# The first addition of a chunk's down products, moved between the two taps of a gate row on VectorE

## The chip, the cores and the metric

The kernel runs on one core of a Trainium2 chip. The metric is the device time of one execution in microseconds (us); the median of repeated executions counts, and lower is better.

## What is computed

One layer of a streaming encoder: an input projection, three token mixers (windowed pooling, a chunked state-space scan, stick-breaking attention), an output projection and layer norm, then a gated channel mixer beside a gated per-layer embedding, and a last layer norm. The change lies in the channel mixer:

```python
def conv_glu_ffn(x, w_up, conv_w, conv_b, w_down):
    up = causal_depthwise_conv(x @ w_up, conv_w, conv_b)     # width 3 along the 1024 tokens
    gate, val = up[..., :D_FF], up[..., D_FF:]               # D_FF = 2816
    return (jax.nn.silu(gate) * val) @ w_down
```

with x of 1024 tokens by 1024 features, all float32.

## The kernel before

The channel mixer's 2816 hidden features are 22 row tiles of 128, taken in 11 chunks (c = 0 to 10) of two tiles, called pp = 0 and 1. A tile needs a gate row (r = 0) and a value row (r = 1), each 128 features by 1024 tokens. The four 512-wide quarters of this up projection come out of seven products (A11, S1, S2, S3, A12, S4, A22: a Strassen scheme), so VectorE has to combine them in PSUM: five `combine` steps per tile. Every product and every down product is a float32 product made of three passes: each operand is held as a rounded part (`hi`) and a rest (`lo`). ScalarE writes the `hi` part of each weight operand (`op_hi`), VectorE the `lo` part (`op_lo`), GpSimd the sums of weight tiles (`weight_sums`).

The program is written by hand, engine by engine, as straight-line queues tied by semaphores. Each engine runs its own queue in order. Chunks 2 to 8 run in a hardware loop (`Fori`), in which the wait values and the columns of the tap weights come from registers; chunks 0, 1, 9 and 10 are written out.

**TensorE** in chunk c (`chunk`, from line 1189): six products of tile 0 (`even`), then the 16 down products of chunk c-1 (`down(c, k)`, k = 0 to 15), then A22 of tile 0, then seven products of tile 1 (`odd`). A down product is two hidden tiles times three passes, six matmuls of 512 columns (L735 to L737 in the profile); a product of `even` or `odd` is twelve (L1094 to L1096). The down products go to four PSUM banks in turn. Down product k, from k = 4 on, therefore waits until addition k-4 has emptied its bank:

```python
if k >= 4:
    eng.wait_ge(dn_added, 16 * (c - 1) + k - 3 + 16 * it)
```

**VectorE** in chunk c runs `chunk` (line 2045 on). `add_down(c, ks, it)` (L1989) adds the down products ks from PSUM to the accumulator `acc` in SBUF; each addition waits for its down product (`dn_full`) and counts up `dn_added`. `taps(c, pp, r, it, parts)` makes the last two taps of the width-3 convolution of one row: part 1 (L1937) waits for ScalarE's first tap (`row_tap`, L1519) and counts up `row_mid`, part 2 (L1941) waits for `row_mid` and counts up `row_done`. Both read PSUM and `conv_ff` (the SBUF buffer `cf`) and write `conv_ff`. `combine` steps 1 to 5 are L1965, L1968, L1971, L1973, L1975; `op_lo` is L603; `glu` L1948; `h_low` L1954.

Who waits for the gate row's `row_done` (`taps(c, 0, 0)`): ScalarE's `silu(c, 0)` (L1525), which stands in ScalarE's queue behind `op_hi` of A11, S1 and S2 of tile 1; and TensorE's first product of chunk c+1.

Of the kernel before, what the change touches and what calls it, by code (L numbers as in the profile page):

```python
# [293 lines left out]
def build(nc, ctx, a, out):  # L294
# [305 lines left out]
    def op_lo(c, o, pp, it=0):  # L600

        nc.vector.wait_ge(op_hi_done, lo_count(c, o, pp) + 18 * it)
        nc.vector.tensor_tensor(op_place(c, o, pp, True), op_raw(c, o, pp), op_place(c, o, pp, False).bitcast(F32),  # L603
                                ALU.subtract).then_inc(op_lo_done, 1)

    def up_row(pp, r):

        b = (Y_BANK if r else X_BANK)[pp]
        return ps[:, b:b + 2, :].rearrange("p b n -> p (b n)")
# [1030 lines left out]
    def _(eng):  # L1640
# [286 lines left out]
        def column(c, step, it):  # L1927
            return par[:, c:c + 1] if isinstance(it, int) else par[:, bass.ds(c + step * it, 1)]

        def taps(c, pp, r, it=0, parts=(1, 2)):  # L1930

            t = 2 * pp + r
            src = up_row(pp, r)
            w = PARAMS["ff_w"] + 3 * (4 * c + t)
            if 1 in parts:
                eng.wait_ge(row_tap, 4 * c + t + 1 + 4 * it)
                v.scalar_tensor_tensor(out=cf[:, r, 1:], in0=src[:, :S - 1], scalar=column(w + 1, 12, it),  # L1937
                                       in1=cf[:, r, 1:], op0=ALU.mult, op1=ALU.add).then_inc(row_mid, 1)
            if 2 in parts:
                eng.wait_ge(row_mid, 4 * c + t + 1 + 4 * it)  # L1940
                v.scalar_tensor_tensor(out=cf[:, r, 2:], in0=src[:, :S - 2], scalar=column(w, 12, it),  # L1941
                                       in1=cf[:, r, 2:], op0=ALU.mult, op1=ALU.add).then_inc(row_done, 1)

        def glu(c, pp, it=0):

            eng.wait_ge(silu_ff, 2 * c + pp + 1 + 2 * it)
            eng.wait_ge(row_done, 4 * c + 2 * pp + 2 + 4 * it)
            v.tensor_tensor(cf[:, 0, :], cf[:, 0, :], cf[:, 1, :], ALU.mult).then_inc(glu_done, 1)  # L1948

        def h_low(c, pp, it=0):  # L1950

            eng.wait_ge(hh_done, 2 * c + pp + 1 + 2 * it)
            h_h, h_l = (h2h, h2l) if c == LASTC else (hh, hl)
            v.tensor_tensor(h_l[pp][:, :], cf[:, 0, :], h_h[pp][:, :].bitcast(F32), ALU.subtract).then_inc(h_done, 1)  # L1954

        def combine(c, pp, step, it=0):

            n = 10 * c + 5 * pp
            x, y = X_BANK[pp], Y_BANK[pp]
            p1, u2 = pu[:, 0, :], pu[:, 1, :]  # L1960
            product = {1: S2, 2: S1, 3: S3, 4: S4, 5: A22}[step]
            eng.wait_ge(prod_full, product_count(c, product, pp) + 14 * it)
            if step == 1:
                eng.wait_ge(p1_done, 2 * c + pp + 1 + 2 * it)
                ins = v.tensor_tensor(u2, p1, ps[:, y + 1, :], ALU.add)  # L1965
            elif step == 2:
                eng.wait_ge(combined, n + 1 + 10 * it)
                ins = v.tensor_tensor(p1, u2, ps[:, x + 1, :], ALU.add)  # L1968
            elif step == 3:
                eng.wait_ge(combined, n + 2 + 10 * it)  # L1970
                ins = v.tensor_tensor(ps[:, y + 1, :], p1, ps[:, y, :], ALU.add)  # L1971
            elif step == 4:
                ins = v.tensor_tensor(ps[:, x + 1, :], u2, ps[:, x + 1, :], ALU.add)  # L1973
            else:
                ins = v.tensor_tensor(ps[:, y, :], u2, ps[:, y, :], ALU.add)  # L1975
            ins.then_inc(combined, 1)

        def add_down(c, ks, it=0):

            first = 16 * (c - 1)  # L1980
            for k in ks:
                j, h = k // 2, k % 2
                eng.wait_ge(dn_full, first + k + 1 + 16 * it)
                dst = acc[:, j, h * HALF:(h + 1) * HALF]
                if k == 0:
                    eng.wait_ge(u_free, 2 * KT)
                    if first:
                        eng.wait_ge(dn_added, first + 16 * it)
                v.tensor_tensor(dst, dst, ps[:, DOWN_BANKS[k % 4], :], ALU.add).then_inc(dn_added, 1)  # L1989
# [38 lines left out]
        def second_half(c, it=0):  # L2028

            op_lo(c + 1, S2, 0, it)  # L2030
            op_lo(c + 1, S3, 0, it)
            combine(c, 1, 4, it)
            op_lo(c + 1, A12, 0, it)
            taps(c, 1, 0, it)
            combine(c, 1, 5, it)
            op_lo(c + 1, S4, 0, it)
            taps(c, 1, 1, it)
            if c + 1 < LASTC:
                op_lo(c + 1, D0A, 0, it)
            glu(c, 1, it)  # L2040
            if c + 1 < LASTC:
                op_lo(c + 1, D1A, 0, it)
            h_low(c, 1, it)

        def chunk(c, it=0):

            combine(c, 0, 1, it)
            combine(c, 0, 2, it)
            op_lo(c, D0B, 0, it)
            combine(c, 0, 3, it)  # L2050
            op_lo(c, D1B, 0, it)
            op_lo(c, A22, 0, it)
            combine(c, 0, 4, it)
            taps(c, 0, 0, it)
            add_down(c, range(5), it)
            op_lo(c, A11, 1, it)
            add_down(c, range(5, 8), it)
            op_lo(c, S1, 1, it)
            op_lo(c, S2, 1, it)
            add_down(c, range(8, 16), it)  # L2060
            op_lo(c, S3, 1, it)
            op_lo(c, A12, 1, it)
            combine(c, 0, 5, it)
            op_lo(c, S4, 1, it)
            taps(c, 0, 1, it)
            op_lo(c, A22, 1, it)
            glu(c, 0, it)
            h_low(c, 0, it)
            op_lo(c + 1, A11, 0, it)
            combine(c, 1, 1, it)  # L2070
            combine(c, 1, 2, it)
            op_lo(c + 1, S1, 0, it)
            combine(c, 1, 3, it)
            second_half(c, it)

        first_chunk()
        second_half(0)
        chunk(1)
        with eng.Fori(0, CHUNKS - 4) as it:
            chunk(2, it)  # L2080
        chunk(LASTC - 1)
        c = LASTC
        combine(c, 0, 1)
# [275 lines left out]
```

## Time and profile before

| | us |
|---|---|
| median of 3 runs | 1300.06 (1298.59 to 1300.7) |
| the profiled execution | 1299.85 |
| its span in the trace | 1298.1 |
| TensorE matmul busy | 1260.1 (97%) |
| VectorE busy | 839.7 (65%) |
| ScalarE busy | 512.9 (40%) |
| GpSimd busy | 232.7 (18%) |
| the 144 additions L1989 on VectorE | 96.1 busy, 685 ns each |
| the 44 taps of part 1 and the 44 of part 2 | 56.4 busy each, 1281 and 1282 ns each |

The span is what the profiler sees of one execution; 1.75 us lie around it. In the trace PE is a matmul, PEld a weight load, DVE VectorE, ACT ScalarE, POOL GpSimd. A time in brackets behind a row is how long the engine was idle before it, and the arrow says what ended that. The end of a matmul is modelled: in a dense stream a matmul of 512 columns is shown with 0.39 us, while the next one starts 0.227 us after it. In the same way the next VectorE instruction starts slightly before the shown end of the one before it.

### The profile page before, as it was taken

The page shows a single profiled execution, that of the slowest core. Times are in us where ns is not written, and L with a number is a line of the kernel's source. Part 1 is how long each engine was busy: PE and PEld are TensorE (multiplying, and loading weights), DVE is VectorE, ACT ScalarE, POOL GpSimd, SP SyncE. Part 2 cuts the span into 40 slices and gives each one's busy share as a digit, 9 for nine tenths or more (in the row PEclk, how much of TensorE's full clock was granted, in tenths as well). Part 3 has the DMA queues.
Part 4 walks back from the last instruction along what each step waited for, and adds up shares of the span by engine and source line. Part 5 has one row for each costly group of instructions (what it writes and reads, how often), then busy time and mean ns, then how long its engine had stood idle before and what let it go on. Part 6 is the DMA issues. An engine that isn't in the chain of part 4 may idle for free.

```text
span 1298.1 us, 16439 instructions
## 1 busy us (share of the span) xinstructions
PE 1260.1 (97%) x6120; PEld 1013.9 (78%) x6120; DVE 839.7 (65%) x1004; ACT 512.9 (40%) x794; POOL 232.7 (18%) x157
## 2 busy tenths in 40 slices
PE   7999999999998999999989999999999999999997
PEld 6777777777876888888868887878788877878886
DVE  5546646646495546625677777767686777687774
ACT  5435545457764225213433342424232423233441
POOL 0000000062300002610311111111111121212127
PEclk9999999999999999999989999999999999999999
DMA  6101101100004122110120211111111212010112
GB/s 240 49 33 37 36 26 46 36 34 17 1 18 136 58 78 84 50 34 17 65 65 33 65 49 48 48 48 65 34 64 51 75 35 65 32 65 33 65 62 117
DMA packets 22804, 71.94 MB, mean 55 GB/s; under 512 B 2528, under 2 KB 2784, under 8 KB 22752
## 3 DMA queue, kind: packets, MB, share of 16 engines
q1 hardware_dynamic: 22752, 71.22, 16.1%
q8 instruction: 36, 0.59, 0.2%
q14 instruction: 16, 0.13, 0.0%
HBM read 67.02 MB, written 4.19 MB: 55 GB/s over the span
## 4 chain that ended last, share of the span: by engine, by line
PE 54%; DVE 16%; issue 7%; ACT 5%; DMA 4%; POOL 2%; DVEq 1%; ACTq 0%; SPq 0%; POOLq 0%
PE ps L735 12%; PE ps L737 12%; PE ps L736 12%; DVE conv_ff L1937 4%; DVE w_lo L603 3%; DMA raw<-u_up 3%; ACT conv_ff L1519 2%; PE ps L1094 2%; PE ps L1096 2%; PE ps L1095 2%; ACT w_hi L598 2%; PE ps L813 1%; PE ps L830 1%; DMA down_raw<-u_down 1%; POOL weight_sums L2251 1%
## 5 line engine op out<-in xcount | busy, mean ns | idle before, releaser
L735 PE MATMUL ps<-x_hi,w_hi 128*128 128x512 f32 x336 | 139.1, 414 | 8.3 <-DVE x_lo L1691 7.3
L1094 PE MATMUL ps<-mix_hi,w_hi 128*128 128x512 f32 x352 | 139.0, 395 | 7.5 <-DVE partial L1968 6.3
L1096 PE MATMUL ps<-mix_hi,w_lo 128*128 128x512 f32 x352 | 138.0, 392 | 0.0
L1095 PE MATMUL ps<-mix_lo,w_hi 128*128 128x512 f32 x352 | 138.0, 392 | 0.0
L737 PE MATMUL ps<-x_hi,w_lo 128*128 128x512 f32 x336 | 132.4, 394 | 0.0
L736 PE MATMUL ps<-x_lo,w_hi 128*128 128x512 f32 x336 | 131.8, 392 | 0.0
L1989 DVE TENSOR_TENSOR acc<-acc,ps 128x512 f32<-128x512 f32 x144 | 96.1, 685 | 49.7 <-PE ps L737 49.0
L2251 POOL TENSOR_TENSOR weight_sums<-raw 128x512 f32<-128x512 f32 x22 | 32.4, 1475 | 480.4 <-DMA raw<-u_up 480.4
L735 PE MATMUL ps<-h_hi,w_hi 128*128 128x512 f32 x288 | 113.2, 393 | 5.2 <-DVE acc L1989 5.1
L736 PE MATMUL ps<-h_lo,w_hi 128*128 128x512 f32 x288 | 112.2, 390 | 0.0
L737 PE MATMUL ps<-h_hi,w_lo 128*128 128x512 f32 x288 | 112.1, 389 | 0.0
L598 ACT ACTIVATE w_hi<-weight_sums 128x512 fp32r<-128x512 f32 x44 | 27.8, 631 | 206.4 <-PE ps L737 157.9
L1094 PE MATMUL ps<-t_hi,w_hi 128*128 128x512 f32 x264 | 102.8, 389 | 0.3 <-DVE ps L1971 0.3
L1096 PE MATMUL ps<-t_hi,w_lo 128*128 128x512 f32 x264 | 102.7, 389 | 0.0
L1095 PE MATMUL ps<-t_lo,w_hi 128*128 128x512 f32 x264 | 102.7, 389 | 0.0
L1519 ACT ACTIVATE conv_ff<-ps,params 128x1024 f32<-128x1024 f32 x44 | 53.1, 1206 | 97.5 <-DVE ps L1975 54.8
L1715 DVE TENSOR_TENSOR_SCAN ps<-ps,zero 128x1024 f32<-128x1024 f32 (+7 forms) x48 | 65.3, 1361 | 33.3 <-ACT ps L1298 33.2
L1094 PEld LDWEIGHTS ps<-mix_hi,w_hi 128*128 128x128 f32 x352 | 66.6, 189 | 24.8 <-DVE partial L1968 5.7
L735 PEld LDWEIGHTS ps<-x_hi,w_hi 128*128 128x128 f32 x336 | 63.7, 189 | 23.9 <-DVE x_lo L1691 7.3
L1096 PEld LDWEIGHTS ps<-mix_hi,w_lo 128*128 128x128 f32 x352 | 66.6, 189 | 14.2
L1937 DVE SCALAR_TENSOR_TENSOR conv_ff<-ps,params,conv_ff 128x1023 f32<-128x1023 f32 x44 | 56.4, 1281 | 33.0 <-ACT conv_ff L1519 32.9
L1095 PEld LDWEIGHTS ps<-mix_lo,w_hi 128*128 128x128 f32 x352 | 66.6, 189 | 13.7
(268 smaller groups left out, 2727.7 us busy)
## 6 DMA issues: line engine op xcount, KB each, us to landing
raw<-u_up SPq DMA_DIRECT2D x44, 512.0 KB, 3.3
raw<-u_in SPq DMA_DIRECT2D x22, 512.0 KB, 3.3
down_raw<-u_down SPq DMA_DIRECT2D x38, 256.0 KB, 2.7
x_stage<-u_x SPq DMA_DIRECT2D x8, 512.0 KB, 8.4
raw<-u_out SPq DMA_DIRECT2D x8, 512.0 KB, 3.2
x_nat<-x_nat SPq DMA_DIRECT2D x8, 512.0 KB, 3.2
raw<-u_gate SPq DMA_DIRECT2D x8, 512.0 KB, 3.3
out<-o_norm SPq DMA_DIRECT2D x7, 512.0 KB, 2.6
```

The costliest lines, as they stand in the source:

```text
L598: nc.scalar.activation(op_place(c, o, pp, False), op_raw(c, o, pp), ACT.Copy).then_inc(op_hi_done, 1)
L735: mm(dst, w_hi, x_hi, start=first, stop=False)
L736: mm(dst, w_hi, x_lo, start=False, stop=False)
L737: return mm(dst, w_lo, x_hi, start=False, stop=last)
L1094: mm(dst, w_h[:, k], t_h[:, kt, :], start=fresh and kt == 0, stop=False, skip_group_check=True)
L1095: mm(dst, w_h[:, k], t_l[:, kt, :], start=False, stop=False, skip_group_check=True)
L1096: last = mm(dst, w_l[:, k], t_h[:, kt, :], start=False, stop=kt == 3, skip_group_check=True)
L1519: act(cf[:, r, :], up_row(pp, r), ACT.Identity, scale=column(w, 12, it), bias=column(b, 4, it)).then_inc(row_tap, 1)
L1715: link(v.tensor_tensor_scan(z[:, ::-1], z[:, ::-1], zero[:, 0:1].broadcast_to([P, keys]), 1.0, ALU.mult, ALU.add))
L1937: v.scalar_tensor_tensor(out=cf[:, r, 1:], in0=src[:, :S - 1], scalar=column(w + 1, 12, it), in1=cf[:, r, 1:], op0=ALU.mult, op1=ALU.add). ...
L1989: v.tensor_tensor(dst, dst, ps[:, DOWN_BANKS[k % 4], :], ALU.add).then_inc(dn_added, 1)
L2251: g.tensor_tensor(t0[:, :], wb[:, 0:HALF], wb[:, HALF:D], ALU.add).then_inc(sum_done, 1)
```

## The change

Within `chunk` on VectorE (chunks 1 to 9), `taps(c, 0, 0)` is split into its two parts, and addition 0 goes between them; additions 1 to 4 follow part 2. No instruction, wait or count is added or removed, and no other queue is touched.

```diff
             op_lo(c, A22, 0, it)
             combine(c, 0, 4, it)
-            taps(c, 0, 0, it)
-            add_down(c, range(5), it)
+            taps(c, 0, 0, it, (1,))
+            add_down(c, range(1), it)
+            taps(c, 0, 0, it, (2,))
+            add_down(c, range(1, 5), it)
             op_lo(c, A11, 1, it)
             add_down(c, range(5, 8), it)
```

## Rows read from the trace of the kernel before

**Rows 1.** The page: TensorE's busy share, granted clock in 40 slices.
```profile
PE 1260.1 (97%) x6120; PEld 1013.9 (78%) x6120; DVE 839.7 (65%) x1004; ACT 512.9 (40%) x794; POOL 232.7 (18%) x157
...
PEclk9999999999999999999989999999999999999999
```

**Rows 2.** Waits of PE: who for whom, us in total, times, longest.
```profile
PE ps L1094 <- DVE partial L1968: 6.3, 8, 4.6
PE ps L735 <- DVE acc L1989: 5.1, 7, 0.9
```

**Rows 3.** Timeline of chunk 3: start us, us, engine, line, operation.
```profile
790.80 1.28 DVE L1937 SCALAR_TENSOR_TENSOR conv_ff<-ps,params,conv_ff 128x1023 f32<-128x1023 f32 x1 [1.69 <-ACT conv_ff L1519]
792.24 1.28 DVE L1941 SCALAR_TENSOR_TENSOR conv_ff<-ps,params,conv_ff 128x1022 f32<-128x1022 f32 x1 [0.15 <-DVE conv_ff L1937]
792.29 0.19 PEld L735 LDWEIGHTS ps<-h_hi,w_hi 128*128 128x128 f32 x1
792.51 0.39 PE L735 MATMUL ps<-h_hi,w_hi 128*128 128x512 f32 x1
792.96 0.39 PE L737 MATMUL ps<-h_hi,w_lo 128*128 128x512 f32 x1
793.44 3.11 DVE L1989 TENSOR_TENSOR acc<-acc,ps 128x512 f32<-128x512 f32 x5
793.89 1.28 POOL L2251 TENSOR_TENSOR weight_sums<-raw 128x512 f32<-128x512 f32 x1 [24.78 <-DMA raw<-u_up]
794.17 0.50 PE L735 MATMUL ps<-h_hi,w_hi 128*128 128x512 f32 x1 [0.82 <-DVE acc L1989]
794.51 0.39 PE L736 MATMUL ps<-h_lo,w_hi 128*128 128x512 f32 x1
795.26 1.30 POOL L2255 TENSOR_TENSOR tables<-weight_sums,raw 128x512 f32<-128x512 f32 x1
796.47 0.69 DVE L603 TENSOR_TENSOR w_lo<-raw,w_hi 128x512 fp32r<-128x512 f32 x1
```

**Rows 4.** Timeline: down product 4 in chunks 2, 7 and 9.
```profile
732.67 0.50 PE L735 MATMUL ps<-h_hi,w_hi 128*128 128x512 f32 x1 [0.47 <-DVE acc L1989]
...
1039.97 0.50 PE L735 MATMUL ps<-h_hi,w_hi 128*128 128x512 f32 x1 [0.88 <-DVE acc L1989]
...
1161.77 0.39 PE L737 MATMUL ps<-h_hi,w_lo 128*128 128x512 f32 x1
1162.25 0.50 PE L735 MATMUL ps<-h_hi,w_hi 128*128 128x512 f32 x1
```

**Rows 5.** The chain of waits, from chunk 3 into chunk 4: start us, us, what.
```profile
813.28 0.24 PE ps L1096
813.54 0.71 DVE ps L1975
...
845.58 0.70 DVE partial L1968
```

**Rows 6.** Timeline of PE where S4 of tile 0 begins, chunk 4.
```profile
845.76 0.39 PE L1096 MATMUL ps<-mix_hi,w_lo 128*128 128x512 f32 x1
846.39 0.49 PE L1094 MATMUL ps<-mix_hi,w_hi 128*128 128x512 f32 x1 [0.25 <-DVE partial L1968]
```

**Rows 7.** Timeline of chunk 1, written out: taps and first additions.
```profile
668.67 1.28 DVE L1937 SCALAR_TENSOR_TENSOR conv_ff<-ps,params,conv_ff 128x1023 f32<-128x1023 f32 x1 [1.28 <-ACT conv_ff L1519]
669.99 1.28 DVE L1941 SCALAR_TENSOR_TENSOR conv_ff<-ps,params,conv_ff 128x1022 f32<-128x1022 f32 x1
```

**Rows 8.** Timeline of ScalarE, chunk 3, behind the gate row's taps.
```profile
799.94 0.63 ACT L598 ACTIVATE w_hi<-weight_sums 128x512 fp32r<-128x512 f32 x1 [8.78 <-PE ps L737]
...
801.00 1.05 ACT L1525 ACTIVATE conv_ff<-conv_ff 128x1024 f32<-128x1024 f32 x1
```

**Rows 9.** Timeline of chunk 2: a lo step beside GpSimd.
```profile
734.02 1.29 POOL L2255 TENSOR_TENSOR tables<-weight_sums,raw 128x512 f32<-128x512 f32 x1
734.97 0.89 DVE L603 TENSOR_TENSOR w_lo<-raw,w_hi 128x512 fp32r<-128x512 f32 x1
```

## The prediction

> **What bounds the kernel now.** I read the page first. TensorE is busy for 97% of the span at a granted clock of nearly full speed throughout (the 2.4 GHz level) [rows 1]. So there is little idle time to win, and the question is which of TensorE's few pauses this edit touches. The view of waits, for TensorE, answers it: in the channel mixer two waits return in nearly every chunk. The down products wait for an addition L1989, seven times, 5.1 us in all, and S4 of tile 0 waits for `combine` step 2 (L1968), eight times, of which one is 4.6 us (in chunk 1) and the other seven (6.3 - 4.6) / 7 = 0.24 us in the mean [rows 2].
>
> Which addition the down products wait for is seen in the timeline of chunk 3 [rows 3]. Four down products run without a break; the last matmul of number 3 starts at 792.96. The first matmul of number 4 would follow 0.227 us later, at 793.19, the spacing of the dense stream (792.51 to 792.96 is two such steps). It starts at 794.17. VectorE began the five additions 0 to 4 at 793.44; five in 3.11 us, with the last shown at its full 0.69 us, means one every 0.605 us. Addition 0 ends at 793.44 + 0.69 = 794.13, and TensorE starts 0.04 us later. So it is addition 0 that TensorE waits for, and addition 0 itself waits for nothing but its place in VectorE's queue: down product 3's last matmul starts at 792.96, so down product 0's last one, three times six matmuls before, started at 788.9. In front of it stand the two taps of the gate row, at 790.80 and 792.24.
>
> **The loss at this place.** In chunk 3 down product 4 starts 794.17 - 793.19 = 0.98 us late. The restart also costs something: the first matmul behind the pause is shown with 0.50 instead of 0.39 us, and the second one comes 0.34 instead of 0.227 us after it [rows 3], 0.11 us more. Together 1.09 us. The view's idle time (0.82) counts from the modelled end of the last matmul, so the loss is that number plus 0.39 - 0.227 = 0.16, plus 0.11: idle plus 0.27. The seven waits are chunks 2 to 8, from 0.47 (chunk 2) to 0.88 us (chunk 7) [rows 4]. Their sum is 5.1 + 7 x 0.27 = 7.0 us, a mean of 1.0 and a largest of 1.15. In chunk 9 the same gap is too short to show as idle: 1161.77 to 1162.25 is 0.48 instead of 0.227, so 0.25 + 0.11 = 0.36 us [rows 4]. In chunk 1 there is no such gap, since TensorE was held up 4.6 us shortly before [rows 2]. Total to be won here: 7.4 us, if nothing new takes the place.
>
> **The change, part by part.** It moves one addition over one tap; counts and durations stay. I write t for the start of part 1 of the taps (790.80 in chunk 3).
>
> Addition 0, moved forward. Back to back, the instruction behind a tap starts 793.44 - 792.24 = 1.20 us after it [rows 3]. So addition 0 starts at t + 1.20 and is done at t + 1.20 + 0.69 + 0.04 = t + 1.93 as TensorE sees it. Before it was t + 3.37. It is 1.44 us earlier: 792.73 in chunk 3, where TensorE's down product 4 is due at 793.19. Its weight load goes 0.22 us ahead of the matmul (792.29 before 792.51), so the wait should be met by 792.97, and is. In chunk 7, with the largest loss, the due time against the taps is 0.06 us sooner: still covered. The pause at down product 4 goes in all eight chunks.
>
> Part 2 of the taps, moved back by 0.605 us less what its own wait cost. In the loop it stands 1.44 us behind part 1 with 0.15 us idle for `row_mid` [rows 3]; in the written-out chunk 1 it is 1.32 us and nothing is shown as idle [rows 7]. With an addition between them the wait is met while VectorE works. So part 2 starts at t + 1.20 + 0.605 = t + 1.80 instead of t + 1.44, 0.36 us later. Who waits for `row_done`: silu (L1525), which runs 801.00, behind an `op_hi` that sat 8.78 us idle for a down product [rows 8]. The row would be done at 790.80 + 1.80 + 1.28 = 793.88, seven us ahead. TensorE's wait for it is in the next chunk. Price nothing; the cover is those seven us.
>
> Additions 1 to 4. Addition 1 starts at t + 1.80 + 1.20 = t + 3.00, done for TensorE at t + 3.73. Before, it was t + 2.64 + 0.605 = t + 3.25: it comes 0.25 us sooner too, by the vanished idle time at the tap. But down product 5 now falls due sooner as well: with loss L at number 4 gone, its first matmul is due at t + 3.37 + 0.11 + 1.36 - L = t + 4.84 - L (1.36 is six steps of 0.227). **Here lies the next wait.** With L = 1.09 it is due at t + 3.75, addition 1 is there at t + 3.73: met, but not the 0.22 us ahead that the weight load wants. I charge what the restart rows show, 0.11 us, so a loss of 3.73 + 0.11 - (4.84 - L) = L - 1.0 where that is positive: 0.15 in chunk 7, 0.09 in chunk 3, little or none elsewhere, 0.3 us in all. If the 0.15 us of idle at the tap remained after all, each of the seven chunks of the loop with a mean L of 1.0 would lose 0.15 more, 0.9 us in all, as the small loss of chunk 2 leaves it free. Down product 6 waits for addition 2, which comes 0.605 us after addition 1 and is due 1.36 us later: free, and so on.
>
> The lo step of A11 (L603, 796.47) stands behind addition 4, which can't start before down product 4 is done (793.19 + 1.36 + about 0.17, so 794.7) nor before t + 3.00 + 3 x 0.605 = 795.62. The lo step then starts at 796.22 instead of 796.47. It now meets GpSimd's L2255 (795.26 to 796.56) [rows 3]. What that does is seen in chunk 2: there the same step started beside L2255 (734.02 to 735.31) and took 0.89 instead of 0.69 us [rows 9]. The worst is that it waits for the whole rest of L2255 and ends at 796.56 + 0.69 = 797.25, 0.34 us late. Bounds 0 and 0.34 us on VectorE; addition 5 behind it then ends by about 798, and down product 9, the one that waits for it, is due at 794.55 + 4 x 1.36 = 800.0. Price on TensorE nothing, and the cover is 2 us.
>
> The Trainium skill (SBUF — State Buffer, section Who interferes with whom) says why: a VectorE instruction with two SBUF inputs contends with a GpSimd instruction that reads SBUF, and is blocked to its end, while one with at most one SBUF input is not. By that rule the lo step would wait until 796.56 and end at 797.25, the two taps and the additions (one tensor from PSUM each) would be untouched, and the sum would be the same. The five additions beside L2251 and L2255 at one per 0.605 us agree with it, and so does the 0.89 in chunk 2, roughly.
>
> **Does the gain last to the end?** What could eat it is a chain of fixed length that starts before the pause and ends behind it, past TensorE. The chain of waits shows what the next chunk hangs on: A22 of tile 0, TensorE's last matmul behind the down products (813.28), then `combine` step 5 (L1975), lo steps, a weight load, the sums, taps, down to step 2 (L1968) at 845.58 [rows 5], where S4 starts with 0.25 us shown as idle, a loss of 0.4 plus 0.11 us [rows 6]. Both this chain and TensorE's own stream start from the same matmul at 813.28, which comes after the down products. If the down products end 1 us sooner, both start 1 us sooner, and S4's pause stays as it is. The trace supports this: the pause at down product 4 varies from 0.47 to 0.88 us over the chunks [rows 4], while those at S4 are 0.24 in the mean, 0.25 in chunk 4 [rows 2, 6]; if it were the pause at S4 that gives way, the two would trade against each other. What is late next is then down product 5 with its few hundredths, and S4 as before. The other transfers and sums are released by counts of lo steps, which in this stretch are paced by TensorE (the 8.78 us of [rows 8]).
>
> The sum: 7.4 - 0.3 = 7.1 us off the profiled execution of 1299.85, hence 1292.8. The median of the runs is 0.2 us above that execution, so 1293.0. With the bound of 0.9 us it is 1293.9; with no new loss at all 1292.7. With the spread of the runs (1298.6 to 1300.7) this case's own range is 1291.5 to 1295.
>
> **The rivals.**
> The gain is won and half of it given back. A chain past TensorE that I took as moving along does not, for instance a weight transfer begun before the down products, and S4's pause grows from 0.5 to about 1 us in each loop chunk. Against it stands the constancy of the S4 pauses. Result 1293.0 + 8 x 0.45 = 1296.6.
>
> The change doesn't do what it says: TensorE's wait isn't ended by addition 0's place in the queue but by something that moves with it (down product 0's own count arriving late). Then addition 0 in its new place would wait as long as before and the time stays 1300. Against it: 0.04 us between the end of addition 0 and the matmul, and no idle time before it.
>
> Slower: contention on VectorE. Part 2 and addition 1 now run where GpSimd's L2251 starts (793.89). If GpSimd held them up as it holds up lo steps, until both its instructions end at 796.56, addition 1 would be ready at 796.56 + 0.69 + 0.04 = 797.29, and down product 5, which ran at 794.17 + 0.11 + 1.36 = 795.64 before, would be 1.65 + 0.11 us later than before: eight times that is +14 us, 1314. It decides against the change once addition 1 is ready later than t + 4.73, 1.0 us behind my estimate. Against it: the five additions ran undisturbed beside the same two instructions [rows 3].
>
> **How the numbers follow.** My case 0.84, half given back 0.07, no effect 0.05, slower 0.04. The likeliest gives 1293.0. The range takes the case with its bounds and reaches toward the half-absorbed one: 1291.3 to 1296.8. 0.2% of the time is 2.6 us, about what a measurement of this kernel can tell from no change. Faster by more (below 1297.5): my case and the half one, 0.90. Within: 0.06. Slower: 0.04.
>
> **What would show it.** In the trace after: in chunk 3 addition 0 starts 1.20 us behind part 1, part 2 0.6 us behind that with no idle shown; the waits of PE for L1989 fall from 5.1 us to under 0.5, and what is left sits at down product 5; a loop chunk lasts 60.4 us, measured between two lo steps of A11, instead of 796.47 - 734.97 = 61.5 [rows 3, 9]; the pauses at S4 stay near 0.24; the lo step of A11 takes up to 1.1 us with no TensorE pause behind it. I am wrong if the pauses at S4 grow by what the down products gained, if a pause of several tenths shows at down product 5, or if the chunk's length falls by less than 0.8 us.

## The result and the profile after

The changed kernel takes 1292.64 us in the median of six runs (1291.07 to 1295.67), against 1300.15 us before (1298.59 to 1300.7). The ratio is 0.9945, with a 95% interval of 0.9932 to 0.9958. A second set of five runs gives the same ratio. The forecast was 1293.0 us.

The page of the changed kernel, the line of the engines:

```profile
span 1290.5 us, 16439 instructions
PE 1257.5 (97%) x6120; PEld 1013.5 (79%) x6120; DVE 838.9 (65%) x1004; ACT 512.8 (40%) x794; POOL 232.4 (18%) x157
```

The same instructions run; the span is 7.6 us shorter. The view of waits, for PE and PEld, answers to [rows 2] (who for whom, us in total, times, longest):

```profile
PE ps L1094 <- DVE partial L1968: 6.3, 8, 4.6
...
PEld ps L735 <- DVE acc L1989: 1.8, 6, 0.5
```

The wait of matmuls for an addition (5.1 us before) has gone from the list; what is left of it is a wait of six weight loads, 1.8 us against 8.6 in eight before. The wait at S4 is unchanged to the tenth. The timeline of chunk 3 answers to [rows 3]:

```profile
788.80 1.28 DVE L1937 SCALAR_TENSOR_TENSOR conv_ff<-ps,params,conv_ff 128x1023 f32<-128x1023 f32 x1 [1.69 <-ACT conv_ff L1519]
790.00 0.68 DVE L1989 TENSOR_TENSOR acc<-acc,ps 128x512 f32<-128x512 f32 x1
790.59 1.28 DVE L1941 SCALAR_TENSOR_TENSOR conv_ff<-ps,params,conv_ff 128x1022 f32<-128x1022 f32 x1
791.20 0.39 PE L735 MATMUL ps<-h_hi,w_hi 128*128 128x512 f32 x1
791.78 2.47 DVE L1989 TENSOR_TENSOR acc<-acc,ps 128x512 f32<-128x512 f32 x4
792.33 0.39 PE L737 MATMUL ps<-h_hi,w_lo 128*128 128x512 f32 x1
792.52 0.19 PEld L735 LDWEIGHTS ps<-h_hi,w_hi 128*128 128x128 f32 x1 [0.22 <-DVE acc L1989]
792.56 0.46 PE L735 MATMUL ps<-h_hi,w_hi 128*128 128x512 f32 x1
793.21 1.29 POOL L2257 TENSOR_TENSOR tables<-weight_sums,raw 128x512 f32<-128x512 f32 x1
794.17 0.88 DVE L603 TENSOR_TENSOR w_lo<-raw,w_hi 128x512 fp32r<-128x512 f32 x1
```

Addition 0 starts 1.20 us behind part 1 of the taps, part 2 follows 0.59 us behind it without the 0.15 us of idle time. Down product 4 starts at 791.20 in a stream without a gap. The new place to look at is down product 5 at 792.56: its weight load waits for addition 1 (791.78 + 0.69 = 792.47). From tap to tap (chunk 3 to 4) a loop chunk now takes 849.41 - 788.80 = 60.61 us, against 61.42 before. Measured as the prediction asks, between the lo steps of A11 in chunks 2 and 3, it is 794.17 - 733.52 = 60.65 us: 0.85 less than before, where 1.1 were forecast for this chunk.

**Where the 7.6 us lie.** The stretch that the change can reach runs from chunk 1's down product 0 to TensorE's last matmul. These two rows of the timeline, for the changed kernel:

```profile
665.49 0.39 PE L735 MATMUL ps<-h_hi,w_hi 128*128 128x512 f32 x1
...
1282.17 0.39 PE L1134 MATMUL ps<-last_w_hi,last_h_lo 128*128 128x512 f32 x1
```

That is 616.68 us. Before, the same two stand at 666.46 and 1289.75, 623.29 us apart. So 6.6 us come from the stretch (0.3 of them because TensorE's first matmuls in it still ran at half the granted clock before, which the last section comes back to). Another 0.97 us were there before it began, in code that is the same, and the 8.3 us behind the last matmul are equal. From here on I compare this stretch first, and the medians beside it. What lies behind the last matmul is 8.3 us in the first three kernels of the table, 9.0 to 9.1 in the next four and 7.9 in the last two, so a median holds that difference too.

| kernel | stretch, us | lost at down products 4 and 5, chunks 2 to 9 | lost at S4, chunks 3 to 9 | median, us |
|---|---|---|---|---|
| before | 623.29 | 7.4 | 3.6 | 1300.15 |
| changed | 616.68 | 0.8 | 3.6 | 1292.64 |
| changed, once more | 616.07 | 0.3 | 3.6 | 1292.12 |
| `late` | 628.64 | 12.2 | 3.7 | 1305.56 |
| `two_between` | 615.80 | 0 | 3.6 | 1291.83 |
| `ahead` | 615.75 | 0 | 3.7 | 1291.65 |
| `tap_last` | 615.58 | 0 | 3.6 | 1292.57 |
| `s4_first` | 614.72 | 3.6 | 0 | 1287.62 |
| `s4_ahead` | 610.84 | 0 | 0 | 1283.51 |

A loss is what the distance between the starts of two matmuls has above 0.227 us, summed where it is over 0.03 us. The median of the kernel before was 1300.15 beside the first set of the changed kernel, 1300.27 beside the second set and the runs up to `ahead`, and 1299.73 beside the last three.

### The profile page after: what moved, and what is told of

Read it like the earlier page. It is cut to its first block, busy times and chain, and to the rows that moved or that the text cites. A ratio compares the mean times of both kernels' runs of the same rounds, so it can differ in the third digit from the quotient of the medians.

```text
span 1290.5 us, 16439 instructions
## 1 busy us (share of the span) xinstructions
PE 1257.5 (97%) x6120; PEld 1013.5 (79%) x6120; DVE 838.9 (65%) x1004; ACT 512.8 (40%) x794; POOL 232.4 (18%) x157
## 4 chain that ended last, share of the span: by engine, by line
PE 60%; DVE 13%; issue 6%; ACT 4%; DMA 2%; POOL 2%; DVEq 0%; ACTq 0%; POOLq 0%; SPq 0%
PE ps L735 13%; PE ps L737 13%; PE ps L736 13%; PE ps L1094 4%; PE ps L1095 3%; PE ps L1096 3%; DVE conv_ff L1937 3%; DMA raw<-u_up 2%; DVE w_lo L603 2%; ACT conv_ff L1519 2%; PE ps L813 1%; PE ps L830 1%; ACT w_hi L598 1%; PE ps L789 1%; POOL weight_sums L2253 1%
## 5 line engine op out<-in xcount | busy, mean ns | idle before, releaser
L736 PE MATMUL ps<-x_lo,w_hi 128*128 128x512 f32 x336 | 132.2, 393 | 0.0
```

What stands on the lines that cost most here:

```text
L736: mm(dst, w_hi, x_lo, start=False, stop=False)
```

## The experiments

**`after_again`: the changed kernel once more**, no edit.

> The changed kernel once more. The trace after shows 6.4 us gone from the tap of chunk 2 to the end, 0.15 in chunk 1, and another 1.0 us that was already there when chunk 1's tap began, in code that the change does not touch. Theory A: that 1.0 us is a variation between executions, the change is worth 6.6 us, so the ratio in time is near 0.9950, and this profile has its chunk 1 tap anywhere between 667 and 669 us. Rival B: the new order shifts something before chunk 1 too, the tap stands at 667.7 again and the ratio is 0.9942.

Median 1292.12 us (1290.55 to 1294.18), ratio 0.9945 (0.9931 to 0.9958). In its profile chunk 1's tap starts at 666.52, against 667.67 in the first profile of the same kernel and 668.67 before. The point moves by 1.1 us between two profiles of one kernel, and in the other kernels with nothing changed ahead of it, it stands between 666.5 and 668.0 (667.80 in `late`, whose edit leaves everything up to this point as before). So theory A holds in that the 1.0 us need no cause in the change. The ratio itself doesn't tell 0.9950 from 0.9942. The stretch was worth 7.2 us this time, mainly since down product 5 lost 0.3 instead of 0.8 us.

**`late`: addition 0 later still**, from the kernel before:

```diff
             taps(c, 0, 0, it)
-            add_down(c, range(5), it)
             op_lo(c, A11, 1, it)
+            add_down(c, range(5), it)
```

> The kernel before, with the lo step of A11 in front of addition 0 as well: addition 0 comes 0.6 us later behind both taps. Theory A (TensorE waits for addition 0's place in the queue, and every tenth lost there is lost to the end): the pause at down product 4 grows by 0.6 us in eight chunks, 4.9 us, so 1305.0 us. Rival B (the pause is ended by something else, or a later wait takes up the shift): no change, 1300.

Median 1305.56 us (1305.10 to 1306.13), ratio 1.0044 (1.0028 to 1.0059): 5.3 us slower, the stretch 5.35 us longer. The timeline of chunk 3:

```profile
792.44 1.28 DVE L1941 SCALAR_TENSOR_TENSOR conv_ff<-ps,params,conv_ff 128x1022 f32<-128x1022 f32 x1 [0.15 <-DVE conv_ff L1937]
793.63 0.68 DVE L603 TENSOR_TENSOR w_lo<-raw,w_hi 128x512 fp32r<-128x512 f32 x1
794.23 3.12 DVE L1989 TENSOR_TENSOR acc<-acc,ps 128x512 f32<-128x512 f32 x5
...
793.11 0.39 PE L737 MATMUL ps<-h_hi,w_lo 128*128 128x512 f32 x1
794.97 0.50 PE L735 MATMUL ps<-h_hi,w_hi 128*128 128x512 f32 x1 [1.47 <-DVE acc L1989]
```

One instruction of 0.60 us more in front of addition 0, and TensorE's idle time goes from 0.82 to 1.47 us [rows 3]. Theory A it is: TensorE waits for addition 0's place in VectorE's queue. The 0.4 us above the expected 4.9 are chunk 1, which I had left out: it had no pause before, and loses 0.64 us at down product 4 here. Every tenth lost at this place is lost to the end, in both directions.

**`two_between` and `ahead`: room for addition 1.** Two ways to have addition 1 ready sooner. `two_between`, from the changed kernel:

```diff
             taps(c, 0, 0, it, (1,))
-            add_down(c, range(1), it)
+            add_down(c, range(2), it)
             taps(c, 0, 0, it, (2,))
-            add_down(c, range(1, 5), it)
+            add_down(c, range(2, 5), it)
```

and, from the changed kernel as well,

```diff
-            taps(c, 0, 0, it, (1,))
             add_down(c, range(1), it)
-            taps(c, 0, 0, it, (2,))
+            taps(c, 0, 0, it)
             add_down(c, range(1, 5), it)
```

> The changed kernel, with addition 1 also between the two taps. The trace after shows a new loss at down product 5 of 0.05 to 0.31 us in six chunks, 0.76 us together, because addition 1 is ready just when its matmul is due. Theory A: addition 1 is now ready 1.2 us sooner, that loss goes, part 2 of the taps is 0.6 us later at no price: 0.7 us faster than the changed kernel. Rival B: part 2 of the taps has a price after all (silu, glu) and the time is the same or longer by up to 0.6 us in each of nine chunks.

> The changed kernel, with addition 0 in front of both taps, where VectorE sits idle 1.7 us for ScalarE's first tap. Theory A: addition 0 is done in that idle time, the pause at down product 4 goes as with the change, and addition 1 comes 2.6 instead of 3.0 us behind the first tap, so down product 5 is free as well: 0.7 us faster than the changed kernel, 1291.9. Rival B: addition 0's wait for down product 0 holds the taps up, in each chunk by up to 0.5 us, and some 4 us of the gain are lost: 1297.

Medians 1291.83 us (1291.62 to 1295.09; ratio 0.9942, 0.9928 to 0.9956) and 1291.65 us (1290.92 to 1292.43; ratio 0.9934, 0.9921 to 0.9948). The medians can't tell these from the changed kernel; the traces can. In both, no matmul of the down products starts late in any chunk, and the stretch is 0.9 us shorter than in the first profile of the changed kernel, 0.3 us shorter than in the second. The expected 0.7 lies between. In `ahead`, addition 0 used the idle time in front of the tap:

```profile
787.74 0.69 DVE L1989 TENSOR_TENSOR acc<-acc,ps 128x512 f32<-128x512 f32 x1 [0.36 <-PE ps L737]
789.08 1.28 DVE L1937 SCALAR_TENSOR_TENSOR conv_ff<-ps,params,conv_ff 128x1023 f32<-128x1023 f32 x1 [0.65 <-ACT conv_ff L1519]
```

It waited 0.36 us for down product 0 (the bracket), and 0.65 us were still idle before the tap. Rival B of `ahead` falls, and so does that of `two_between`, whose stretch is shorter and not longer.

**`tap_last`: the cover of part 2 tried out.**

```diff
             taps(c, 0, 0, it, (1,))
-            add_down(c, range(1), it)
+            add_down(c, range(5), it)
             taps(c, 0, 0, it, (2,))
-            add_down(c, range(1, 5), it)
```

> The changed kernel, with part 2 of the gate row's taps behind all of additions 0 to 4. Theory A (part 2 has some seven us of cover before silu): its row is done about 3 us later than with the change and nothing waits for it; additions 1 to 4 come 1.2 us sooner, so no loss at down product 5. From chunk 1's down product 0 to TensorE's last matmul: 615.8 us, as with addition 1 between the taps, 0.3 to 0.9 less than with the change. Rival B: the later row end is felt at silu, and what follows it, in every chunk: 617 or more.

Median 1292.57 us (1290.81 to 1293.26), ratio 0.9946 (0.9929 to 0.9962); stretch 615.58 us. Part 2 and who needs it, chunk 3:

```profile
792.27 1.28 DVE L1941 SCALAR_TENSOR_TENSOR conv_ff<-ps,params,conv_ff 128x1022 f32<-128x1022 f32 x1
...
795.74 0.64 ACT L598 ACTIVATE w_hi<-weight_sums 128x512 fp32r<-128x512 f32 x1 [7.81 <-PE ps L737]
796.28 0.62 ACT L598 ACTIVATE w_hi<-tables 128x512 fp32r<-128x512 f32 x1
796.80 1.05 ACT L1525 ACTIVATE conv_ff<-conv_ff 128x1024 f32<-128x1024 f32 x1
```

The row ends at 793.55, silu runs at 796.80, right behind two `op_hi`, of which the first waited for a down product. So part 2 has cover of 3.2 us even here. With the change it ends at 790.59 + 1.28 = 791.87 and silu runs at 798.03, so the cover is 6.2 us. Theory A holds.

**`s4_first`: the other pause taken away alone**, from the changed kernel:

```diff
# second_half(c), on VectorE; the same two are taken out where chunk c+1 began
+            combine(c + 1, 0, 1, it)
+            combine(c + 1, 0, 2, it)
             h_low(c, 1, it)
# chunk(c), and the written-out last chunk
-            combine(c, 0, 1, it)
-            combine(c, 0, 2, it)
```

> The changed kernel, with steps 1 and 2 of combine for chunk c+1 in front of h_low(c, 1) on VectorE, for the pause at S4 that the change left untouched (0.51 us in eight chunks). Theory A: step 2 comes 1.3 us sooner, the pause at S4 goes, but the taps stay where they are against the matmul A22 of tile 0, so TensorE reaches down products 4 and 5 0.5 us sooner than the additions allow: at least 0.4 of each 0.5 us is lost again there, and only chunk 1, with its long pause at S4, keeps about 1.2 us. 1291.0. Rival B: the pauses at S4 and at the down products are independent, all 4 us and the 1.2 of chunk 1 are kept: 1287.

Median 1287.62 us (1286.56 to 1288.83), ratio 0.9908 (0.9891 to 0.9924). In chunk 3:

```profile
787.92 0.50 PE L735 MATMUL ps<-h_hi,w_hi 128*128 128x512 f32 x1
788.26 0.40 PE L736 MATMUL ps<-h_lo,w_hi 128*128 128x512 f32 x1
...
789.19 0.39 PE L737 MATMUL ps<-h_hi,w_lo 128*128 128x512 f32 x1
789.71 0.50 PE L735 MATMUL ps<-h_hi,w_hi 128*128 128x512 f32 x1
```

Down product 5 starts 0.52 instead of 0.227 us behind the matmul before it, and the restart adds 0.11. In chunks 3 to 9 the 3.6 us lost at S4 are gone, and 3.6 us are lost at down products 4 and 5, where it was 0.3 to 0.8: over the loop theory A is what happened, the two pauses trade, and some 0.4 to 0.9 us are kept. As a time my 1291.0 was still a miss by 3.4 us, and 1287.62 is near the 1287 of rival B: the median alone would have spoken for the wrong theory. Chunk 1 and the last chunk made the difference: the long wait at S4 of chunk 1 falls from 4.6 to 2.9 us, and from chunk 9's down product 0 to the last matmul it takes 132.2 instead of 133.0 us. There it isn't S4 that gains, which in the last chunk has no pause in either kernel, but A22 of the second tile. In the changed kernel it waits for `combine` step 3 (L1971):

```profile
1228.79 0.50 PE L1094 MATMUL ps<-t_hi,w_hi 128*128 128x512 f32 x1 [0.45 <-DVE ps L1971]
```

It starts 0.61 us late and pays 0.11 more; in `s4_first` the wait is gone, and nothing takes its place. In chunk 1 the shorter wait also shortened what follows it. After it TensorE runs at half the granted clock for a while, which the windows of the kernel before show (pause, S4, first down products; columns: stretch, length, then PE, PEld, DVE, ACT, POOL, and behind them the clock):

```profile
656.00:661.00 5.00, 0.61 (x3) 0.18 (x1) 4.38 (x6) 1.06 (x1) 0.00 (x0) 0.92 0.30 99
661.00:666.40 5.40, 5.22 (x12) 4.12 (x13) 2.62 (x5) 1.67 (x3) 0.00 (x0) 0.50 0.19 52
```

From the first matmul of this S4 to down product 0 it is 666.46 - 661.18 = 5.3 us before, and 662.63 - 658.28 = 4.35 us in `s4_first`: in a dense stream at the full clock it is 2.7. In the two profiles of the changed kernel it is 5.2 and 5.0, and in all seven profiles with the 4.6 us of wait between 4.95 and 5.3. So chunk 1 gives 1.7 us of wait and 0.6 to 0.8 us of slow clock. With 0.4 to 0.9 from the loop and 0.8 at the end that makes 3.5 to 4.2 of the 4.5 to 5.0 us; another 0.4 lie behind the last matmul (7.9 instead of 8.3 us), and I know no cause for them.

**`s4_ahead`: both pauses.** As `s4_first`, and on VectorE:

```diff
-            taps(c, 0, 0, it, (1,))
             add_down(c, range(1), it)
+            taps(c, 0, 0, it, (1,))
+            add_down(c, range(1, 2), it)
             taps(c, 0, 0, it, (2,))
-            add_down(c, range(1, 5), it)
+            add_down(c, range(2, 5), it)
```

> As the run before it, and addition 0 in front of both taps, addition 1 between them, so that down products 4 and 5 have room. Theory A: the pause at S4 goes (4.1 us), the one at the down products stays away, chunk 1 keeps 1.2 us: 5 us faster than the changed kernel, 1287.3, and a loop chunk of 59.9 us. Rival B: h_low, now 1.2 us later, holds up down product 0 or the lo steps behind it, and the loop chunk stays at 60.4 us or more.

Median 1283.51 us (1282.61 to 1283.91), ratio 0.9875 (0.9859 to 0.9892) to the kernel before: the fastest of all. Its page, and busy time by engine in four windows of one chunk each (length, then PE, PEld, DVE, ACT, POOL with their counts, clock, DMA):

```profile
span 1280.8 us, 16446 instructions
...
661.90:721.74 59.84, 59.84 (x266) 49.56 (x265) 46.97 (x59) 20.10 (x28) 11.00 (x8) 1.00 0.16 53
721.74:781.58 59.84, 59.84 (x266) 49.57 (x265) 44.26 (x55) 20.04 (x28) 10.96 (x8) 1.00 0.17 53
781.58:841.42 59.84, 59.84 (x266) 49.56 (x265) 44.97 (x57) 20.13 (x29) 11.49 (x8) 1.00 0.17 53
841.42:901.26 59.84, 59.84 (x266) 49.57 (x265) 45.37 (x57) 19.89 (x28) 10.97 (x8) 1.00 0.16 53
```

TensorE is busy for every hundredth of the chunk. 59.84 us is 264 matmuls at 0.227 us: nothing is left to win in a loop chunk by moving VectorE's work. The stretch is 5.2 us shorter than the changed kernel's second profile, and the loop chunk is the 59.9 us expected, so rival B falls. As a time the 1287.3 was a miss by 3.8 us: the median fell by 8.6. The two profiled executions, 7.9 us apart, show what I left out. The stretch gives 5.2; in front of it 2.3 are gained, of which 1.7 are the wait at S4 of chunk 1 (2.9 instead of 4.6) and some 0.7 the shorter time at half the clock behind it, of which I had counted 1.2 in all; and 0.4 lie behind the last matmul, with no cause known.

## Why the prediction was right

**The bound and the loss.** TensorE's pauses were read as what they are. The 7.4 us (the table, counted from matmul starts, has the same) went, and `late` showed the same mechanism in the other direction: 0.60 us of VectorE work in front of addition 0 cost 5.3 us in all.

**Addition 0.** Predicted at t + 1.20, seen at 790.00 - 788.80 = 1.20 us behind part 1. There is no pause at down product 4 in any chunk of either profile of the changed kernel.

**Down product 5, the next wait.** Named rightly, sized too low for that execution. Predicted 0.3 us in all, half of it in chunk 7. The first profile shows 0.8, the second 0.3. In the first, chunk 4 reads:

```profile
852.87 0.39 PE L737 MATMUL ps<-h_hi,w_lo 128*128 128x512 f32 x1
853.13 0.50 PE L735 MATMUL ps<-h_hi,w_hi 128*128 128x512 f32 x1
853.47 0.40 PE L736 MATMUL ps<-h_lo,w_hi 128*128 128x512 f32 x1
```

The first matmul of number 5 is 0.03 us late, yet the second stands 0.34 us behind it, the full 0.11 of the restart. I had let that 0.11 fade out with L - 1.0. In the chunks of the two profiles that lose anything here, the second matmul pays 0.04 to 0.11 us, and the full 0.11 in six of ten, also where the first is late by 0.04 or less. That is the term that was mis-sized, by up to 0.5 us. The largest loss, 0.31 us in chunk 7 of the first profile (0.13 in the second), comes near the several tenths that I had named as a sign of being wrong. `two_between` and `ahead` took the loss away in full, so its cause is shown.

**The idle time at part 2.** It vanished as worked out (0.59 from addition 0 to part 2), in every loop chunk. The upper bound that kept it is dropped.

**Silu and part 2.** Priced at nothing, and `tap_last` shows it with half the cover gone. The cover with the change was 6.2 us and not seven, since silu, which hangs on a down product, comes sooner as well.

**The lo step of A11 beside GpSimd.** It starts at t + 5.37 (794.17 - 788.80; predicted 5.42) and takes 0.88 us instead of 0.69, in chunk 2 1.05 us; in `late`, where it started at 793.63, before GpSimd's pair at 794.05, 0.68. No TensorE pause follows. Its partner on GpSimd ran from 793.21 to 794.50, and the step ended at 795.05, 0.55 us behind it. That 0.55 is no accident: in the nine profiles of this document 366 lo steps were lengthened beside a GpSimd instruction, to between 0.73 and 1.80 us, and every one of them ended 0.54 to 0.56 us behind that instruction. The 0.89 of chunk 2 before fits as well (735.31 + 0.55 = 735.86). So the step is held to the very end of GpSimd's instruction, as the prediction took from the Trainium skill (SBUF — State Buffer, section Who interferes with whom); only the time behind that end is 0.55 and not the 0.69 that I had added, so my worst case was 0.14 us too long. In the written-out chunk 9 little of GpSimd's instruction had passed, and the step took 1.56 us, more than the 1.1 that I had named as the most, again with no TensorE pause behind it. Who starts first decides: in `late` the step wasn't lengthened, but the GpSimd instruction that started behind it took 1.40 instead of 1.28 us. The four additions in 2.47 us, one each 0.60, were untouched beside the same GpSimd instructions, and the slower rival falls with them.

**The gain lasts.** S4's pause stayed at 6.3 us in eight waits. That the chain past TensorE starts from the same matmul as TensorE's own stream fits two results: removing the pause at down product 4 left S4's as it was, and removing S4's (`s4_first`) brought the other back, because the taps hang on that chain and the additions behind them. In the prediction I had taken the even pauses at S4 as a sign that the two don't trade. Here they do, but in one direction only: the pause behind the taps' place went without a price, and most of the one ahead of it came back.

**The sum.** 7.1 us forecast; 6.6 and 7.2 us in the stretch, of which 0.3 each are the clock of its first matmuls before and not the change; 7.5 and 8.2 us in the medians of the two sets. The part of the medians above 7.2 isn't explained by the change and is within the interval (4.2 to 6.8 thousandths, 5.5 to 8.8 us). That the forecast of 1293.0 stands within 0.4 us of 1292.64 is therefore partly luck: the loss at down product 5 was larger than forecast, and an execution that ran 1.0 us ahead before the stretch began made up for it.

## What to carry to other kernels

When the bounding engine waits for a buffer, look at what stands in front of the freeing instruction in the other engine's queue: an instruction that everybody can wait for (here a tap with several us of cover) belongs behind one that the bounding engine needs now. Each freed pause moves the next deadline forward by its own length, so work out the margin of the next buffer too, and count it from the weight load, not the matmul. Where two pauses lie on one loop, removing one may only lengthen the other; here one alone kept 0.4 to 0.9 of 3.6 us in the loop, and both together all of it.

## What the runs showed of the hardware

A wait that is met just in time can cost TensorE 0.11 us all the same: in chunk 4 of the changed kernel the first matmul started 0.03 us late, and the second stood 0.34 instead of 0.227 us behind it. In the other chunks that lost anything at this place the second matmul paid between 0.04 and 0.11 us. The pauses in the loop never cost clock: from 725 to 1150 us, where they lie, the granted clock is 1.00 (2.4 GHz) in the kernel before, and in `late` too with its pauses of up to 1.5 us. The one long pause, 4.6 us at S4 of chunk 1, did: in the kernel before, the 12 matmuls behind it ran at a granted clock of 0.50 (1.2 GHz), one per 0.43 us, and the first of the down products with them; with a pause of 2.9 us (`s4_first`, `s4_ahead`) it fell as well, but six or seven matmuls later it was back. I had not counted this stretch at all.

A lo step, which reads two SBUF operands on VectorE and started behind a GpSimd `tensor_tensor` that was still running, ended 0.55 us behind that instruction in all 366 cases; the 474 additions that started beside one, with one operand in PSUM, kept their 0.67 to 0.69 us.

Between executions of identical code the start of the channel mixer's chunk 1 moved by 1.1 us, nearly a tenth of a per cent of the whole, and more than some edits are worth. A stretch between two fixed instructions told apart versions that the medians of four to six runs could not.
